# Compressed attention branch: block rows of keys and values laid out together, scores waiting for the keys only, rope tables moved to a feed-forward part

## The reference, cut to what matters

```python
def compress(kv, pos_emb, w1, b1, w2):            # once for keys (kc), once for values (vc)
    idx = jnp.arange(n_cmp)[:, None] * CMP_STRIDE + jnp.arange(CMP_BLOCK)[None, :]   # 15 blocks of 32 rows
    blocks = kv[:, idx] + pos_emb[None, None, :, None, :]
    flat = blocks.transpose(0, 1, 3, 2, 4).reshape(B, n_cmp, G, CMP_BLOCK * D)       # 4096 wide
    return jax.nn.silu(flat @ w1 + b1) @ w2
...
    k_cmp = compress(kc, *cmp_k); v_cmp = compress(vc, *cmp_v)
    k_cmp = partial_rope(k_cmp, cmp_end)
    # per block of 128 queries and group of 4 heads
    s_c = jnp.einsum('btghd,bngd->bghtn', qblk, k_cmp) * scale                       # 15 keys
    p_c = masked_softmax(s_c, cmp_end[None, :] <= t[:, None], -1)
    o_c = jnp.einsum('bghtn,bngd->btghd', p_c, v_cmp)
    # two more branches over all 256 keys, and a gated sum of the three
...
    # second block: angles of three rope tables from `positions`, and one lambda per layer
    lam = jnp.exp(jnp.sum(lp[0] * lp[1])) - jnp.exp(jnp.sum(lp[2] * lp[3])) + lambda_init
```

## Time and profile before

| | |
|---|---|
| median of 3 runs | 2326.73 us (2326.03 to 2326.78) |
| the profiled execution | 2322.58 us |
| its span in the profile | 2320.8 us |
| mean granted TensorE clock | 0.974 of full speed |
| TensorE matmul busy | 2156.6 us, 93% of the span |
| VectorE, ScalarE, GpSimd busy | 1374.7, 997.3, 101.8 us |
| moved | 356.84 MB, 154 GB/s |

### The profile page before, as it was taken

How to read it: one execution, slowest core, us unless ns; L and a number is a source line. 1 busy time by engine, 2 the same in 40 slices (tenths; PEclk the granted TensorE clock), 3 DMA queues, 4 the chain that set the end, 5 groups by cost and what they waited for, 6 DMA issues and landing times.

```text
span 2320.8 us, 29712 instructions
## 1 busy us (share of the span) xinstructions
PE 2156.6 (93%) x12707; PEld 1891.4 (81%) x12707; DVE 1374.7 (59%) x1667; ACT 997.3 (43%) x1324; POOL 101.8 (4%) x121
## 2 busy tenths in 40 slices
PE   6989898889889999899989999999999998999998
PEld 5868787878877899778868789989987877877997
DVE  4656775746666654655676465555565566754544
ACT  4434544524543533344534353444343454443432
POOL 0100010100010000000000000000000000000000
PEclk9989999989989999999999999999999999999999
DMA  6343233443223655435446265555544344543652
GB/s 249 108 161 126 91 109 131 143 148 127 92 77 120 220 191 178 165 109 164 145 145 218 91 205 193 183 192 184 187 157 150 120 160 174 179 152 120 204 189 92
DMA packets 192412, 356.84 MB, mean 154 GB/s; under 512 B 8284, under 2 KB 85144, under 8 KB 192280
## 3 DMA queue, kind: packets, MB, share of 16 engines
q1 hardware_dynamic: 189400, 344.46, 43.9%
q0 software_dynamic: 2880, 10.49, 1.4%
HBM read 353.87 MB, written 1.05 MB: 153 GB/s over the span
## 4 chain that ended last, share of the span: by engine, by line
PE 78%; DVE 12%; ACT 4%; issue 3%; DMA 1%; POOL 1%; SPq 0%; POOLq 0%; ACTq 0%; DVEq 0%
PE bank L1852 14%; PE bank L1848 14%; PE bank L1858 14%; PE bank L1875 7%; PE bank L1872 7%; PE bank L1878 7%; DVE raw_r L2322 4%; PE bank L1896 3%; PE bank L2016 2%; PE bank L1913 2%; ACT high L2125 2%; PE bank L1934 1%; PE bank L1887 1%; POOL stat L2812 1%; PE bank L1904 1%
## 5 line engine op out<-in xcount | busy, mean ns | idle before, releaser
L2322 DVE TENSOR_TENSOR raw_r<-raw,high 128x2048 fp32r<-128x2048 f32 (+1 forms) x308 | 696.5, 2278 | 101.6 <-ACT high L2125 101.6
L2125 ACT ACTIVATE high<-raw 128x2048 fp32r<-128x2048 f32 (+1 forms) x308 | 581.3, 1896 | 273.6 <-PE bank L1858 227.2
L1848 PE MATMUL bank<-high,units_r 128*128 128x512 f32 x1648 | 664.5, 403 | 21.4 <-DVE units L2778 11.8
L1852 PE MATMUL bank<-high,units_r 128*128 128x512 f32 x1648 | 652.0, 396 | 23.9 <-DVE units_r L2343 12.4
L1858 PE MATMUL bank<-raw_r,units_r 128*128 128x512 f32 x1648 | 444.2, 392 | 0.2
L1872 PE MATMUL bank<-units_r,high 128*128 128x256 f32 x1600 | 399.5, 286 | 0.0
L1875 PE MATMUL bank<-units_r,high 128*128 128x256 f32 x1600 | 396.1, 284 | 0.0
L1852 PEld LDWEIGHTS bank<-high,units_r 128*128 128x128 f32 x1648 | 314.7, 191 | 92.1 <-DVE units_r L2343 15.6
L1848 PEld LDWEIGHTS bank<-high,units_r 128*128 128x128 f32 x1648 | 314.1, 191 | 89.0 <-issue 21.8
L1858 PEld LDWEIGHTS bank<-raw_r,units_r 128*128 128x128 f32 x1648 | 312.6, 190 | 67.3 <-DVE raw_r L2322 1.7
L1875 PEld LDWEIGHTS bank<-units_r,high 128*128 128x128 f32 x1600 | 308.2, 193 | 1.2
(11 more groups left out here) (247 smaller groups left out, 1871.3 us busy)
## 6 DMA issues: line engine op xcount, KB each, us to landing
raw<-in_ffn_w_dram SPq DMA_DIRECT2D x132, 1024.0 KB, 5.1
raw<-in_w_in_dram SPq DMA_DIRECT2D x108, 1024.0 KB, 5.0
raw<-in_w_out_dram SPq DMA_DIRECT2D x24, 1024.0 KB, 4.9
raw<-in_cross_wkv_dram SPq DMA_DIRECT2D x16, 1024.0 KB, 5.1
raw<-in_w_branch_dram SPq DMA_DIRECT2D x12, 1024.0 KB, 4.9
raw<-in_cross_wq_dram SPq DMA_DIRECT2D x8, 1024.0 KB, 5.2
raw<-in_cross_wo_dram SPq DMA_DIRECT2D x8, 1024.0 KB, 4.9
raw<-in_w_in_dram SPq DMA_DIRECT2D x4, 832.0 KB, 4.3
```

The source lines that it names most:

```text
L1848: pe.matmul(o, h.high(k0 + k)[:, span], p.hi[k][:, cols], start=start and k == 0, stop=False, skip_group_check=True)
L1852: pe.matmul(o, h.low(k0 + k)[:, span], p.hi[k][:, cols], start=False, stop=False, skip_group_check=True)
L2125: done = act.activation(high, raw, ACT.Copy)
L2322: done = dve.tensor_tensor(low, raw, high.bitcast(F32), ALU.subtract)
```

## The change

Three edits. In `compress()` the rows of keys and of values are laid out first, both of them, each into a buffer of its own, and the projections' buffer is given back then; the two halves of products follow, each as before. In `nsa(g)` the start and the scores wait for the keys only, and the wait for the values stands ahead of the first product with them. `tables()` is cut in two: the bounds stay in the first layer, lambdas, angles and rope tables go beside the first feed-forward part of the second block, one step before each step of that part. The buffer `lam_in` is kept until then.

```diff
@@ compress()
+            es = []
             for which in range(2):
...
                 do("cmp_rows", name=C, src=cc.ap[:, which * 512:which * 512 + 512], e4=e4, posg=posg,
                    need=[cc_end, ("gT",)], after=e.after)
+                es.append((e, e4))
+                yield
+            U.give(cc, ("cmp_rows", f"{N}.cmp1"))
+            yield
+            for which in range(2):
+                C = f"{N}.cmp{which}"
...
+                e, e4 = es[which]
                 b = B.take()
...
-            U.give(cc, ("cmp_rows", f"{N}.cmp1"))
@@ nsa(g)
-            while q_made[g] is None or len(kc_made) < 2:
+            while q_made[g] is None or not kc_made:
                 yield "stuck"
...
-                        krhs, k_need, bias = kcs[:, g * 16:g * 16 + 15], kc_made, cst(f"cmp{t}")
+                        krhs, k_need, bias = kcs[:, g * 16:g * 16 + 15], kc_made[0:1], cst(f"cmp{t}")
...
+                    while len(kc_made) < 2:
+                        yield "stuck"
                     acc, pr = plan.pv(S_, res, 4, vf, P, [*v_made, *kc_made], None if br == 0 else acc, br == 0, br == 2)
@@
-        streams = [compress(), nsa(0), nsa(1), recurrence()] + ([tables()] if l == 0 else [])
+        streams = [compress(), nsa(0), nsa(1), recurrence()] + ([lower_bounds()] if l == 0 else [])
@@
-    def drive(gen):
+    def drive(gen, side=iter(())):
         while True:
+            next(side, None)
             try:
                 next(gen)
@@
-        seam = drive(ffn(l, seam, "ffn1"))
+        seam = drive(ffn(l, seam, "ffn1"), tables() if l == 0 else iter(()))
```

More of the change, by code:

```diff
@@ L812, in make_plan, with lower_bounds @@
         off += 4 * hf
-    def tables():
+    def lower_bounds():
         do("bounds", phase=0, lbs=lbs)
@@ L821, in tables @@
         do("bounds", phase=3, lbs=lbs)
+    def tables():
         for l in range(2):
@@ L942, in compress @@
             cc, cc_end = st_["cc"], cc_made[0]
+            es = []
             for which in range(2):
                 C = f"{N}.cmp{which}"
-                w1, w2 = (A["cmp_w1_k"][l], A["cmp_w2_k"][l]) if which == 0 else (A["cmp_w1_v"][l], A["cmp_w2_v"][l])
                 posg = (G_PK if which == 0 else G_PV) + 32 * l
@@ L950, in compress @@
                    need=[cc_end, ("gT",)], after=e.after)
+                es.append((e, e4))
[4 more added lines that the diff above has]
+                C = f"{N}.cmp{which}"
+                w1, w2 = (A["cmp_w1_k"][l], A["cmp_w2_k"][l]) if which == 0 else (A["cmp_w1_v"][l], A["cmp_w2_v"][l])
+                e, e4 = es[which]
                 b = B.take()
```

## The result

The changed kernel takes 2272.34 us in the median of 4 runs (2271.64 to 2277.84); the kernel before, run beside it, 2326.76 us. The ratio is 0.9771, with a 95% interval of 0.9754 to 0.9788: 2.3% faster, where 1.7% was forecast. A second comparison (run e11) gave 0.9777, 0.9764 to 0.9791.

The account below looks back on a forecast made before the run. TensorE, busy for 93% of the span, was taken as the bound. From the profiled 2322.6 us: - 34.7 (early waits and clock) + 1.0 (keys) + 0.8 (seam) - 6 (late half) = 2283.7, + 4.15 to the median = 2288 us; range 2276 to 2308.

Parts of the forecast that it names:

- The early waits: Compressed branch, both layers: TensorE's waits of 12.8 us at the first product and 10.8 us at the scores go whole.
- Their slow clock: Rows behind those waits return to full clock: 6.2 us for products, 1.8 for scores, 3.1 for pairwise products, 11.1 in all.
- The keys' step: Keys' copy on VectorE now stands behind a split and the rows: adds 1.0 us over both layers, bounds 0 and 2.
- The seam: Start of the first feed-forward part: moved tables delay the second tile's products, adding 0.8 us, bounds 0 and 2.
- the rest of the tables: Tables beside the first feed-forward part, apart from its seam: nearly all hidden under TensorE; at most about 8 us if not.
- The late half: Attention behind the first scores, both layers: of 41.8 us lost to idle time and clock, 6 us go; bounds +15, -10.
- The walk over the waits: Late attention stretches followed wait by wait in the new order: about 29.5 of 41.8 us left, a gain of 12.
- The step to the median: Whole kernel: 4.15 us added because the median of the runs lay that far above the profiled execution.
- The late half gives 10 us back: Rival: the late attention waits for VectorE, so time gained early is lost there; 2306 us, chance 0.24.
- loads did not come late: Rival: the values' weights land late in the compression, so their product still waits; 2302 us, chance 0.06.
- the scores did not wait for the keys' copy: Rival: scores still wait, as the keys' copy comes late; only 19 us go, 2304 or 2305 us, chance 0.06.
- `lam_in` and the buffers: Rival: buffers held longer in the attention make some 30 takes stall, 1.5 us each; slower, 2333 us, chance 0.04.

Follow-up runs that it names:

- e11: The changed kernel unaltered, run and profiled once more: 2272.35 us, ratio 0.9777 to the kernel before.
- e2: The kernel before with only the rows of keys and values laid out together; scores still wait for both, tables stay: 2295.93 us, ratio 0.9872.
- e3: The kernel before with only the wait for the values taken out of the scores (start of `nsa(g)` relaxed too): 2308.20 us, ratio 0.9929.
- e7: The changed kernel with lambdas, angles and rope tables 16 steps later in the first feed-forward part, past its seam: 2272.23 us, ratio 0.9780.
- e5: The changed kernel, order kept, with eleven copies of turned probabilities back on the engines they had before: 2276.49 us, ratio 0.9799.
- e6: The kernel before, order kept, with eleven copies of turned probabilities on the engines the changed kernel gives them: 2327.64 us, ratio 1.0015.
- e9: The kernel before with three empty turns ahead of the compression, giving the changed kernel's order of steps in the late half: 2313.55 us, ratio 0.9954.
- e8: The changed kernel with the forget gate of the second half of heads one step later: 2266.63 us, ratio 0.9757.
- e14: The kernel before, unaltered, executed with a profile once more: 2325.31 us, ratio 1.0001.
- e4: The kernel before with both edits of the attention, tables left beside the first layer: 2275.53 us, ratio 0.9787.
- e12: Both edits of the attention with the tables left in the first layer (e4 again), run beside the changed kernel: 2274.32 us, ratio 0.9784.
- e1: The kernel before with only the tables moved to the first feed-forward part, attention as it was: 2320.04 us, ratio 0.9982.
- e10: The changed kernel with tables 16 steps later, the second half of heads' forget gate one step later and its decay another step later: 2262.21 us, ratio 0.9732.
- e13: e10 with the three bound products of the second layer's forget gate one step later too: 2259.95 us, ratio 0.9721.

## Why the prediction was wrong, by its own steps

**The early waits: right.** Both went whole, 12.8 + 10.8 = 23.6 us, and for the reason given: the rows are ready before the first product, and the second product covers the way of the keys. The waits for the rows go in e2 and stay in e3. Those of the scores all but go in either; only with the second edit do they go without new waits for the gates.

**Their slow clock: right.** Forecast 6.2 us for the products, measured 34.8 - 28.7 = 6.1. Scores: 1.8 against 9.5 - 7.9 = 1.6. The pairwise products: 3.1 against 58.2 - 55.1 = 3.1. Together 10.8 where 11.1 was forecast. In the windows around both compressions the granted clock is now 1.00, not 0.90 and 0.88. The rule of the Trainium skill, "TensorE: Matmul & The Clock Gate", section Terms, gave an estimate of 15.4 us for the windows of before. The rows measure 10.8, less than the rule: of about 31 us at the half level there TensorE was busy in about 23, counted in windows of 1 us.

**The keys' step: too high by a little.** 1.0 us was added for both layers; no wait came.

**The seam: right.** 0.8 us forecast, 0.86 measured with e7, though only 0.22 of it as a wait, where a wait of about 1 us was to show. That the rest of the tables is hidden held too.

**The late half: the step that failed.** The walk over the waits gave 12 us less, idle time and clock together, and I took half: "It rests on durations that shift when anything does". The idle time alone fell by 11.5 us. To that comes the clock: in windows of 1 us TensorE stood 30.8 us at the half level in these stretches before, and 17.1 us after, worth at most (30.8 - 17.1) / 2 = 6.8 us, and 5.8 us if each window counts by how busy TensorE was in it. So the term was 17 to 18 us where -6 stood, outside its bound of 15. The mechanism was half right. Order decides these waits, and the engines of the copies, which I had named as well, don't (e5, e6). The reason given for the new order, that the scores start earlier, isn't needed either: in e3 they start without their wait and the late idle time stays at 30.4 us, in e9 they start later and it falls to 18.9. Of the two waits named, that of 3.34 us went, and the one that I walked to "about 3.3" came out as 3.04, at the place and on the engine named. Halving the walk cost 6 us of the miss. The walk itself was another 5 to 6 us short; its other waits are not on record, so where it was short stays open.

**A cost of the clock that the sum has no term for.** At the end of the second layer both kernels have the same two waits, 0.87 and 2.32 us, ahead of L1848 and L1852 in the old numbers. Before, the clock stayed full behind them; in the changed kernel it fell to 0.57 over the 8 us behind, so that the products up to the next wait ended 2.8 us later against those ahead of it:

```profile
684.63 0.47 PE L1860 MATMUL bank<-high,units_r 128*128 128x512 f32 x1 [0.87 <-ACT units_r L2154]
...
687.42 0.79 PE L1864 MATMUL bank<-high,units_r 128*128 128x512 f32 x1 [2.32 <-DVE units_r L2355]
```

```profile
686.00:694.00 8.00, 6.58 (x17) 5.19 (x18) 1.36 (x2) 0.00 (x0) 0.00 (x0) 0.57 0.00 0
```

The busy time agrees: 10.8 + 6.8 - 2.8 = 14.8 us less by these terms, or 13.8 with the lower value for the late half, and 14.7 measured. And the span: 23.6 + 11.5 idle, 0.4 at a pairwise product of the recurrence (1.16 to 0.73 us), 14.7 busy make 50.2 of the 50.1 us.

**The step to the median: wrong by 4.3 us.** I added 4.15 us, the distance of the profiled execution to the median of three runs. The changed kernel has no such distance (2272.50 and 2272.34). The kernel before took 2321.2 to 2329.1 us in its later executions, with medians of 2324.3 to 2325.3: the three first runs lay high in its spread and the profiled one low. Added up, 11.2 us of the miss are the late half less the new cost and the small terms, 4.3 us are this step. Without the 4.15 us the range would have begun at 2271.9, just under the measured 2272.3.

**The rivals.** None of the four came. "The late half gives 10 us back" was refuted with the opposite sign, loads did not come late (no wait at all at L1946), the scores did not wait for the keys' copy (no wait at L1908 on `short_keys`), and `lam_in` and the buffers cost nothing that a wait of TensorE shows.

## What to carry to other kernels

Where engines work through a fixed list, look for what stands ahead of a short instruction on which the bound engine waits. Putting such an instruction ahead of 2 to 4 us of work that is wanted later (the forget gate, the scan with its decay) was worth more here than the choice of the engine. When a walk through the new order gives a number for each wait, put that number into the sum and not half of it, write each wait down, and add the clock behind the waits that go. When parts of a change are measured apart, look at which waits each part removes: here two parts remove the same one, and a sum that fits does not make them independent. A profiled execution and a median of three runs are two draws from a spread of 8 us here; work out differences within one of them, and don't carry the distance over.

## What the runs showed of the hardware

The same wait does not always bring the clock down. Behind the waits of 0.87 and 2.32 us at the end of the second layer the granted clock stayed full in the kernel before and in e2, e3, e5, e7, e8 and e14, and fell in the changed kernel, e4, e9, e11 and e12 (most) and in e1, e6, e10 and e13 (less), though the program and the waits are the same there in all. It came back alike in both profiles of the changed kernel (e11) and in both of the kernel before (e14). Behind the same two waits at the end of the first layer the clock fell in all sixteen profiles. What decides it no run shows. It is worth up to 2.8 us at one place, and this can hide or feign an edit of 1 us.
